# One subtraction of 1024 columns in place of two of 512, for each block of weights

## What is computed

```python
# first block
h = rmsnorm(x, g_norm1)
proj = h @ w_in
y_a = mla_branch(proj, ...) @ w_o_mla          # 8 heads, w_uq and w_ukv inside
y_b = diff_branch(proj, ...) @ w_o_diff        # 8 heads, difference of two softmaxes
gates = sigmoid(proj[..., OFF_GATE:] + b_gate)
merged = gates[..., :D_MODEL] * y_a + gates[..., D_MODEL:] * y_b
x = x + merged @ w_out
x = x + peer_ffn(rmsnorm(x, g_norm2), w_q_peer, sub_keys, expert_u, expert_v)  # 16384 experts, top 16 of 8 heads
x = rmsnorm(x, g_final)
# second block, layer 0 (retention and convolution) and layer 1 (attention over a window of 128)
x = x + even_mixer(rms_norm(x, ...), ev_w_in, conv_w, ev_w_out)
x = x + odd_mixer(rms_norm(x, ...), od_w_in, ..., od_w_out)
```

## Time and profile before

| | |
|---|---|
| median of three runs | 2863.57 us |
| the profiled execution, its own time | 2867.21 us |
| its span in the trace | 2865.4 us |
| TensorE busy | 2844.4 us (99%) |
| VectorE busy | 2153.7 us (75%) |
| ScalarE busy | 1606.2 us (56%) |
| GpSimd busy | 783.6 us (27%) |
| TensorE's share of the chain that ended last | 97% |
| granted TensorE clock, whole span | 1.00 |
| mean HBM traffic | 227 GB/s |

### The profile page before, as it was taken

How to read it: one execution, slowest core, us unless ns; L and a number is a source line. 1 busy time by engine, 2 the same in 40 slices (tenths; PEclk the granted TensorE clock), 3 DMA queues, 4 the chain that set the end, 5 groups by cost and what they waited for, 6 DMA issues and landing times.

```text
span 2865.4 us, 44533 instructions
## 1 busy us (share of the span) xinstructions
PE 2844.4 (99%) x14126; PEld 2376.1 (83%) x14126; DVE 2153.7 (75%) x3840; ACT 1606.2 (56%) x3235; POOL 783.6 (27%) x531
## 2 busy tenths in 40 slices
PE   8999999999999999999999999999999999999999
PEld 7888788888888888888888888888788888887777
DVE  5568778756888888866768888888866686678775
ACT  5445564555565565655555555555654345556764
POOL 0000000000058786777026665664100000000000
PEclk9999999999999999999999999999999999999999
DMA  7787555466577787778879999999666556664355
GB/s 247 254 259 232 164 170 174 153 188 207 175 195 197 197 197 194 196 197 200 291 257 340 387 365 376 380 390 357 224 206 191 169 176 184 197 184 155 125 158 181
DMA packets 217121, 651.09 MB, mean 227 GB/s; under 512 B 51680, under 2 KB 60640, under 8 KB 216128
## 3 DMA queue, kind: packets, MB, share of 16 engines
q1 hardware_dynamic: 150064, 539.89, 58.5%
q0 software_dynamic: 57376, 104.73, 12.7%
q10 hardware_dynamic: 9520, 4.50, 0.5%
HBM read 627.95 MB, written 21.07 MB: 227 GB/s over the span
## 4 chain that ended last, share of the span: by engine, by line
PE 97%; DVE 1%; DMA 0%; ACT 0%; issue 0%; SPq 0%; DVEq 0%; ACTq 0%
PE bank L1057 19%; PE bank L783 15%; PE bank L787 15%; PE bank L784 15%; PE bank L1062 9%; PE bank L1151 4%; PE bank L1152 4%; PE bank L1146 4%; PE bank L1148 4%; PE bank L1147 4%; PE bank L754 1%; PE bank L1260 0%; PE bank L1283 0%; PE bank L1270 0%; DVE lo L1869 0%; DMA hall<-in_x 0%
## 5 line engine op out<-in xcount | busy, mean ns | idle before, releaser
L1355 ACT ACTIVATE hi<-raw 128x512 fp32r<-128x512 f32 (+1 forms) x1810 | 1120.3, 630 | 951.7 <-PE bank L787 584.3
L1869 DVE TENSOR_TENSOR lo<-raw,hi 128x512 fp32r<-128x512 f32 (+2 forms) x1671 | 1203.5, 734 | 547.9 <-ACT hi L1355 401.7
L1057 PE MATMUL bank<-xt,hi 128*128 128x512 f32 x2304 | 780.1, 394 | 0.0
L783 PE MATMUL bank<-hi,xt 128*128 128x512 f32 (+1 forms) x1924 | 764.2, 397 | 0.0
L784 PE MATMUL bank<-hi,xt 128*128 128x512 f32 (+1 forms) x1924 | 749.1, 389 | 0.0
L1062 PE MATMUL bank<-xt,lo 128*128 128x256 f32 x2304 | 607.5, 277 | 0.0
L787 PE MATMUL bank<-lo,xt 128*128 128x512 f32 (+1 forms) x1924 | 592.8, 389 | 1.1 <-DVE lo L1869 1.1
L1057 PEld LDWEIGHTS bank<-xt,hi 128*128 128x128 f32 x2304 | 427.8, 188 | 94.9
L585 POOL DMA_INDIRECT gates_scratch<-picked,place x256 | 416.9, 1629 | 268.0 <-DVE picked L2422 158.7
L1062 PEld LDWEIGHTS bank<-xt,lo 128*128 128x128 f32 x2304 | 423.6, 188 | 5.6
L787 PEld LDWEIGHTS bank<-lo,xt 128*128 128x128 f32 x1924 | 361.1, 188 | 79.4 <-DVE lo L1869 2.9
(11 more groups left out here) (271 smaller groups left out, 2180.4 us busy)
## 6 DMA issues: line engine op xcount, KB each, us to landing
raw<-in_w_u SPq DMA_DIRECT2D x256, 512.0 KB
raw<-in_w_v SPq DMA_DIRECT2D x140, 512.0 KB
raw<-in_w_ein SPq DMA_DIRECT2D x128, 512.0 KB
hall<-in_w_v SPq DMA_DIRECT2D x116, 512.0 KB, 6.5
raw<-in_w_oin SPq DMA_DIRECT2D x72, 512.0 KB
raw<-in_w_att SPq DMA_DIRECT2D x64, 512.0 KB
raw<-in_w_gate SPq DMA_DIRECT2D x64, 512.0 KB
raw<-in_w_out SPq DMA_DIRECT2D x32, 512.0 KB
```

Source lines behind the costliest of these rows:

```text
L783: pe.matmul(acc[t], xh[t], h_[:, s], start=first, stop=False)
L1057: return pe.matmul(acc[:, :], h_[:, s], xt[:, qp_tile(k)].rearrange("p w t -> p (w t)"), start=first, stop=False)
L1355: act.activation(hi[d][:, c], raw[s][:, c], ACT.Copy).then_inc(hi_ready, 2 // parts)
L1869: dve.tensor_tensor(lo[d][:, c], raw[s][:, c], hi[d][:, c].bitcast(F32), ALU.subtract)\
```

## The change

`split` on VectorE makes one instruction of a whole block instead of two of its halves, wherever it made two. It then waits for `hi_ready` of both halves (and in `w_u` for `block_used` of both), and raises `lo_ready` by 2 at its end. ScalarE still writes `hi` in two halves, and TensorE's instructions and waits stay as they are. Blocks that were subtracted whole before, those of `w_v` after its first and the first eight of the program, stay so. 762 blocks change.

```diff
-            def split(b, i=None, per=0, width=BLOCK, parts=2):
+            def split(b, i=None, per=0, width=BLOCK, parts=1):
...
-                        split(b + q, i, 2 * nb, width if q < nb - 1 else BLOCK, 1 if width < BLOCK and q < nb - 1 else 2)
+                        split(b + q, i, 2 * nb, width if q < nb - 1 else BLOCK)
...
-            split(0, width=640, parts=1)
+            split(0, width=640)
...
-                split(b, parts=1)
+                split(b)
...
-                split(b + 1, parts=1 if j + 1 < N_EXPERT_TILES else 2)
+                split(b + 1)
```

## The result

The changed kernel takes **2942.27 us**, median of 6 runs (2938.88 to 2949.87), against 2865.41 us (2863.45 to 2866.4, 6 runs) before: ratio 1.0272, 95% interval 1.0262 to 1.0282. It is 76.9 us slower. I had forecast 2866.9 us, at most 2871.5. The profiled execution took 2949.87 us, its span is 2948.1 us; that of before took 2867.21, so there are 82.7 us to explain in the two traces.

A forecast was written before the change was run, and what follows sets the result against it. TensorE, busy 2844.4 of 2865.4 us, was taken as the bound, with VectorE hidden nearly everywhere. Terms of 3.0 + 0.1 + 0.2 = 3.3 us on the median 2863.57 gave 2866.9 us, range 2861.5 to 2871.5.

The forecast's parts named there:

- the claim on `w_u`: In `w_u`, low parts come 0.85 us before TensorE asks, 0.45 if VectorE arrives late; zero cost taken.
- Rival A: VectorE becomes late in `w_u` too: 16 spots of 0.5 us, 8 us on top, 2875 us; chance 0.16.
- Its counterargument: In `w_u`, VectorE idles 133.5 us for TensorE's line 1062 before these subtractions, so it catches up quickly.
- Rival B: VectorE's saving wins: its four waits of 4.6 us and the restarts behind them go, 2859.0 us; chance 0.04.
- Rival C: TensorE's restarts and late starts are absorbed and places share one delay: 0 to 1.5 us; chance 0.22.
- The terms in the dense stages: Places outside `w_u` where TensorE's low part comes too late, 3.0 us in sum.
- From `w_uq` to the start of `w_ob`: Late low parts: `w_uq` 0.34 and 0.4, `w_ukv` 0.33, start of `w_ob` 0.5 us.
- the start of `w_ein`: Two late low parts, at 2072.69 and 2079.80, less one gain of 0.07: 0.9 us.
- block 9 of `w_att`: Low part ready later, matmul at 58.75 against 58.30, plus a slower restart: 0.56 us.
- the reload: Loads of `raw` are issued 0.53 us later; three waits in `w_att`, bounds 0 and 1.5, 0.2 us taken.
- The waits of line 787: TensorE's waits on `lo` grow from 1.1 us in 3 to some 3 to 4 us in 8 or 9.
- The saving: VectorE's 762 single subtractions save 120 us of busy time, but only 0.07 us of queue per back-to-back pair.

The follow-up runs named there:

- experiment 7: The changed kernel with two subtractions of 512 columns again in all of `w_u`: 2877.44 us.
- experiment 1: The changed kernel with halves again in the first 176 slots of `w_u`, beside the routing: 2897.69 us.
- experiment 3: The changed kernel, but in the 176 routing slots of `w_u` two subtractions of 512, both behind the whole block's waits and released together: 2893.28 us.
- experiment 8: The changed kernel with two subtractions of 512 columns again in all of `w_u`, `w_gate` and `w_oin`: 2871.12 us.
- experiment 2: The kernel before the change, with whole subtractions of 1024 only in the 176 routing slots of `w_u`: 2904.57 us.
- experiment 4: The changed kernel, but in the 176 routing slots of `w_u` four subtractions of 256, all behind the whole block's waits: 2890.71 us.
- experiment 5: The changed kernel, routing slots of `w_u` in two late halves released together, second input a PSUM bank from slot 20 on: 2891.8 us.
- Experiment 9: The changed kernel with halves in all of `w_u`, those of its first 40 slots behind whole-block waits and released together: 2878.73 us.
- Experiment 10: The changed kernel with halves in all of `w_u`, those of the other 136 routing slots (from the 40th) late and released together: 2879.04 us.

## Why the prediction was wrong, point by point

- **The step that failed** is the claim on `w_u`: "In `w_u` the busiest slots remain covered ... Zero is taken." I checked there only whether TensorE would find its low part ready, and that much held: up to the stall the changed kernel's TensorE takes the same time over `w_u` as before, to within 0.1 us. What I never read was the third engine. POOL's busy time was in the earlier trace rows, 783.6 us, and I did not ask whether GpSimd, which shares `w_u` with these subtractions, minds their length. That was worth 71.5 of the 82.7 us in the profiled execution, the slowest of the six: the wait of 68.7, and 2.8 for a slow restart. By the medians, with experiment 7, it is 65 of 77 us. This is TensorE by stretch around the stall (window, length, busy, clock as a share of full, DMA share, GB/s):

```profile
1355.00:1370.00 15.00, 15.00 (x88) 1.00 0.68 187
1370.00:1430.00 60.00, 5.71 (x34) 0.57 0.23 19
1430.00:1450.00 20.00, 5.55 (x17) 0.50 0.67 206
1450.00:1475.00 25.00, 25.00 (x145) 1.00 0.74 237
```

  After 70 us almost without work the granted clock is 0.50, that is 1.2 GHz, and 17 matmuls take 5.55 us, where at the full 2.4 GHz 88 take 15.00; so they cost some 2.7 us more.
- **Could the trace of before have told?** Yes. Its scatters spread from 1413 to 2062 ns with one shape and one size, and the 46 that took over 1850 ns all began under a subtraction of 0.69 us. A subtraction that is 0.53 us longer makes a held scatter 0.53 us longer, and more of them are held, 136 over 1.85 us in place of 46; an estimate with half of 256 is already 68 us. The slack at `gate(0)` was small against it: the scatters ended at 1351.8, the gates are there 7.6 us after that (1434.6 to 1442.2 in the changed kernel), and VectorE reached line 2085 at 1365.0, so 5.6 us. The changed kernel closes with it: 82.8 us, less 5.6, less the 6.5 us by which VectorE itself comes later to `gate(0)` (1371.5), is the wait of 70.7. I had priced the change only for the engines in its diff.
- **Rival A** named the right row ("waits of line 1057 on `lo` in `w_u`") and the wrong mechanism. It put 16 spots of 0.5 us there; there was one of 68.7. Its counterargument, that VectorE idles 133.5 us and catches up, is true and doesn't help, since idle time of VectorE does not give GpSimd its microseconds back. Rival B did not show: no wait got shorter by VectorE's 84 us. Rival C was not it either.
- **The terms in the dense stages** were right in kind and too small in size. From `w_uq` to the start of `w_ob` I had 1.57 us (0.34 + 0.4 + 0.33 + 0.5), and TensorE's work takes 2.3 us longer there; the start of `w_ein` 0.9 against 1.1. For block 9 of `w_att` I had 0.56 us and 0.2 for the reload, and TensorE's work takes 1.7 us longer there (1.3 to 4.2 in experiments 1, 3, 7 and 8; 0.0 in experiment 2, which has halves there). ScalarE's longest wait for a transfer of `w_att` is 3.5 us before, 3.3 in experiment 2, and 4.1 to 5.7 in these. So the late transfer seems to have landed later, and the 0.2 was too little. The waits of line 787 came out as forecast, 3.8 us in 9.
- **A smaller step that failed**: I listed only places where TensorE waits for `lo`. I wrote that what stands behind VectorE's subtraction would be 0.53 us later and then costed none of it. Lines 2131 and 2788 stand there, and TensorE waits for both: 5.0 us in `w_gate` and some 2.4 to 2.7 in `w_oin`, more than my whole sum. `w_oout` costs 1.1 us at places that my list does not have. Without `w_u`, `w_gate` and `w_oin` (experiment 8) the change costs 5.6 us (3.4 to 8.6), where I had 3.3. In TensorE's work, 71.5 us in `w_u` and 14.5 at all places elsewhere make 86.0 us; the profiled execution shows 82.7 because its first 50 us happened to be 3.3 us shorter than before, as they are in experiment 2 too (3.5).
- **The saving** was sized well: "a pair back to back gives back only 0.07 us". The rows after show it: the subtraction at 296.90 takes 1.23 us and the next instruction starts at 298.04, 1.14 us after it, where a pair held the queue for 1.21. The time of none of the ten kernels lies below that of before, and none of the findings points to one that would: before has no wait left on a subtraction that a longer one could shorten.

## What to carry to other kernels

When an instruction gets longer, look at the engines that run beside it, not only at those that wait for it: an instruction with one size and a wide spread of durations may be held by something. Here its maximum minus its minimum was about the length of what held it: 0.65 us with subtractions of 0.69, 1.19 with those of 1.23. Beside a serial chain of 256 short issues on GpSimd, VectorE instructions with two SBUF inputs were better short (1.63 us a scatter against 2.00), even though VectorE itself saves by long ones. And for each engine whose instruction moves later, list all the products behind it, not just the one that the edit is about.

## What was not expected of the hardware

**GpSimd's indirect scatters are held by a running VectorE subtraction whose two inputs are in SBUF**, from 1.42 to up to 2.60 us, as shown, and one with a single SBUF input does not hold them (1.56 us at most in 60). They can fall into step with the subtractions: over half of them, 136 of 256, then took over 1.85 us, where it was 46 before.

**TensorE has two steady rhythms in `w_u`.** In experiments 3, 4 and 5 TensorE's work from 700 to 1350 us took 11.1 us longer than before, while no wait of TensorE in `w_u` was over 1.1 us; over the whole of `w_u` it was 12.7 to 14.2 us. The group of line 1057 in 850 to 1150 us, of experiment 7 and then of experiment 3:

```profile
L1057 PE MATMUL bank<-xt,hi 128*128 128x512 f32 x866 | 300.3, 394 | 0.0
```

```profile
L1057 PE MATMUL bank<-xt,hi 128*128 128x512 f32 x850 | 300.4, 399 | 0.0
```

The clock is full in both. In this window the hi matmuls start alternately 343 or 344 and 350 ns apart in the first, and 349, 350 and 361 ns in turns of three in the second, without an exception. (Experiment 9 has the quick pace in a third form, 346 or 347 ns each time.) The kernel before has the slower rhythm too, from 760 to 775 us, and leaves it at the next gap. In experiment 4 one can see it set in, at 812.61 (TensorE's timeline; the distance of two starts of line 1057 is 0.35 before it, then 0.39 and 0.43):

```profile
811.87 0.39 PE L1057 MATMUL bank<-xt,hi 128*128 128x512 f32 x1
...
812.22 0.40 PE L1057 MATMUL bank<-xt,hi 128*128 128x512 f32 x1
...
812.61 0.48 PE L1057 MATMUL bank<-xt,hi 128*128 128x512 f32 x1
...
813.04 0.40 PE L1057 MATMUL bank<-xt,hi 128*128 128x512 f32 x1
```

VectorE is done with the four quarters of a block at 812.46, 0.15 us before that matmul starts, so a late low part may be what set it off; no run shows it. The slower rhythm stays until TensorE's wait of 1.1 us, some 560 us later, and goes back there. In experiment 3 a wait of 0.5 us at the same place did not end it. Experiment 10 shows that late low parts by themselves don't cost this, and the one slower run of experiment 9 hints that a kernel can fall into either. What in TensorE makes two rhythms of the same instructions, and which gaps switch it, stays open.
